# Linear attention: the stage between stick-breaking and the chunk solver is dissolved

## The reference

```python
# stick-breaking group: 8 heads of 64
o = stick_breaking_attention(q, k, v)
o = o * rsqrt(mean(o * o, axis=-1) + RMS_EPS) * sb_out_g           # head norm
# linear group (RWKV-7): 8 heads of 64, token-shifted inputs
r, k, v, xw, xa, xg = split(um)
decay = exp(-exp(-softplus(-(w0 + tanh(xw) @ w2)) - 0.5))
a = sigmoid(a0 + xa @ a2);  g = sigmoid(xg) @ g2                   # g: gates
kk = unit(k * k_k);  k = k * (1 + (a - 1) * k_a)
out = rwkv7_scan(r, decay, k, v, kk, a)    # S = S diag(w) - (S kk)(kk a)^T + v k^T ; o = S r
out = groupnorm(out) * ln_w + ln_b
bonus = sum(r * k * r_k, axis=-1) * v
out = (out + bonus) * g
h = h + concat([o_sb, out]) @ w_out
```

## Time and profile before

| | us |
|---|---|
| runs | 1440.41, 1447.54, 2522.86 (median 1447.54) |
| profiled execution | 1440.73 |
| its span, first to last instruction | 1439.0 |
| TensorE busy | 1280.1 (89%) |
| VectorE busy | 568.4 (40%) |
| ScalarE busy | 479.1 (33%) |
| GpSimd busy | 139.4 (10%) |

### The profile page before, as it was taken

One profiled execution on the slowest core, in us unless ns is written; L12 is line 12 of the kernel. 1 busy time (PEld: TensorE's weight loads), 2 busy tenths in 40 slices (PEclk: granted clock), 3 DMA queues, 4 the chain that ended last, 5 costly groups with the idle time before them and its releaser, 6 DMA issues. The chain is left out here.

```text
span 1439.0 us, 24362 instructions
## 1 busy us (share of the span) xinstructions
PE 1280.1 (89%) x10299; PEld 992.4 (69%) x10299; DVE 568.4 (40%) x1026; ACT 479.1 (33%) x808; POOL 139.4 (10%) x202
## 2 busy tenths in 40 slices
PE   5999979799969589987881999999989979899988
PEld 5886845599848455544441998888867868666668
DVE  3335422655462323321225323444448754522232
ACT  4333366602243301110114234555545534111130
POOL 4000023000000022322210001222100000000000
PEclk9999999999979789998895999999999989999999
DMA  4422000000148579999975545223161035113021
GB/s 147 124 88 88 1 1 0 9 4 4 61 139 320 193 254 389 386 384 394 404 296 185 139 139 103 89 89 91 55 88 59 31 142 184 57 59 117 0 68 50
DMA packets 92488, 195.53 MB, mean 136 GB/s; under 512 B 9510, under 2 KB 73084, under 8 KB 79452
## 3 DMA queue, kind: packets, MB, share of 16 engines
q1 hardware_dynamic: 86604, 183.48, 37.4%
q0 software_dynamic: 5200, 8.40, 1.8%
q10 hardware_dynamic: 576, 2.10, 0.4%
HBM read 184.74 MB, written 16.81 MB: 140 GB/s over the span
## 5 line engine op out<-in xcount | busy, mean ns | idle before, releaser
L1784 PE MATMUL hidden_ps<-w_gate,gathered_t 128*64 128x256 f32 x432 | 116.3, 430 | 24.4 <-DMA w_up<-exp_w_up_dram 24.4
L1784 PE MATMUL hidden_ps<-w_up,gathered_t 128*64 128x256 f32 x432 | 116.3, 430 | 0.0
L1784 PEld LDWEIGHTS hidden_ps<-w_gate,gathered_t 128*64 128x64 f32 x432 | 64.7, 155 | 62.8 <-issue 34.1
L613 DVE TENSOR_TENSOR w_in_low<-w_in_raw,w_in_high 128x2048 fp32r<-128x2048 f32 x20 | 45.8, 2292 | 116.8 <-ACT w_in_high L605 116.8
L565 PE MATMUL proj_ps<-block_in_high,w_in_low 128*128 128x512 f32 x232 | 90.5, 390 | 0.0
L565 PE MATMUL proj_ps<-block_in_low,w_in_high 128*128 128x512 f32 x232 | 90.5, 390 | 0.0
L565 PE MATMUL proj_ps<-block_in_high,w_in_high 128*128 128x512 f32 x232 | 90.4, 390 | 0.0
L1347 PE MATMUL wo_ps<-w_out_high,wo_x_high 128*128 128x256 f32 x256 | 75.2, 294 | 16.6 <-DVE w_out_low L613 16.6
L565 PE MATMUL gate_ps<-block_in_high,gate_w_high 128*128 128x512 f32 x192 | 79.6, 415 | 11.1 <-DVE gate_w_low L613 11.1
L565 PE MATMUL gate_ps<-block_in_low,gate_w_high 128*128 128x512 f32 x192 | 76.6, 399 | 0.0
L565 PE MATMUL gate_ps<-block_in_high,gate_w_low 128*128 128x512 f32 x192 | 76.4, 398 | 0.0
(11 more groups left out here) (457 smaller groups left out, 3102.7 us busy)
## 6 DMA issues: line engine op xcount, KB each, us to landing
w_gate<-exp_w_gate_dram SPq DMA_DIRECT2D x27, 1024.0 KB
w_up<-exp_w_up_dram SPq DMA_DIRECT2D x27, 1024.0 KB
w_down<-exp_w_down_dram SPq DMA_DIRECT2D x27, 1024.0 KB
w_in_raw<-w_in_dram SPq DMA_DIRECT2D x20, 1024.0 KB, 5.6
slot_scratch_and_keys<-w_in_dram SPq DMA_DIRECT2D x14, 1024.0 KB, 5.4
vb<-w_in_dram SPq DMA_DIRECT2D x6, 1024.0 KB, 5.6
gate_w_raw_odd<-w_in_dram SPq DMA_DIRECT2D x6, 1024.0 KB, 5.8
slot_scratch_and_keys<-exp_w_gate_dram SPq DMA_DIRECT2D x5, 1024.0 KB
```

Source lines behind the costliest of these rows:

```text
L613: dve.tensor_tensor(self.part[1][n % 2], self.slot(n), self.part[0][n % 2], ALU.subtract).then_inc(self.low, 1)
L1784: x = pe.matmul(g_bank[e % 2][a * CAP:(a + 1) * CAP, 0:DE], xT[e % 2][:, k, :], w[:, k, :], start=(k == 0), stop=(k == KC - 1))
```

## The change

`rwkv_features` is gone as a stage. Its work goes to four places, in the same amounts:

- First projection: `exps` (ScalarE, behind the split of the last weights) and `operands` (VectorE, behind the keys) form `kr`, the bonus products r k r_k (in place of r) and the scaled keys (in place of k). `kr` lies where the raw weights were, and now keeps all keys ahead of all rows.
- Stick-breaking: VectorE scales `bh` first; TensorE sums the bonus between the scores of head 0 and head 1, in the banks of the values; the norms of output tiles 0 and 1 are computed around heads 5 to 7. Outputs go to `mixT` directly.
- Solver: norms of tiles 2 and 3. The solver's scratch is a tile of its own. The gate weights are loaded here.
- Output stage: the gate matmuls stand behind rounds 1 to 4 of the recurrence, their copies on ScalarE.

`HeadNorm` is a new class with one method for each step of a norm.

```diff
             s.sem("early_" + n) for n in ("lora_product", "sigmoids_stored", "kk_log", "kk_rstd", "vector_step"))
+        self.ex = s.sem("early_decay_exps")
...
         self.step(dve, dve.tensor_tensor(rate, kkn, rate, ALU.mult))
+    def exps(self, act, raw_free):
+        H = self.H
+        act.wait_ge(self.dv, FT + 3)
+        act.activation(H["sig"], H["sig"], ACT.Exp, scale=-DECAY).then_inc(self.ex, 1)
+        act.wait_ge(*raw_free)
+        act.activation(H["kr"][:, 1].rearrange("p i t -> p (i t)"), H["cum"].rearrange("p f t -> p (f t)"), ACT.Exp, scale=-DECAY).then_inc(self.ex, 1)
+        act.activation(H["cum"], H["cum"], ACT.Exp, scale=DECAY).then_inc(self.ex, 1)
+        act.activation(H["mid"], H["ends"], ACT.Exp, scale=-0.5 * DECAY).then_inc(self.ex, 1)
+    def operands(self, dve):
+        H, r = self.H, self.um[:, 0:FT, :]
+        c4 = lambda x: x.rearrange("p f (c t) -> p (f c) t", t=P)
+        dve.wait_ge(self.ex, 1)
+        dve.tensor_tensor(H["kr"][:, 0], c4(H["kkn"]), c4(H["sig"]), ALU.mult).then_inc(self.dv, 1)
+        dve.wait_ge(self.ex, 2)
+        self.n += 1
+        self.step(dve, dve.tensor_tensor(H["kr"][:, 1], c4(r), H["kr"][:, 1], ALU.mult))
+        for f in range(FT):
+            dve.scalar_tensor_tensor(out=r[:, f, :], in0=r[:, f, :], scalar=par_col(self.const, PARAM_AT["rw_r_k"] + f),
+                                     in1=self.k[:, f, :], op0=ALU.mult, op1=ALU.mult).then_inc(self.dv, 1)
+        self.n += FT
+        dve.wait_ge(self.dv, self.n)
+        dve.wait_ge(self.ex, 3)
+        dve.tensor_tensor(self.k, self.k, H["cum"], ALU.mult).then_inc(self.dv, 1)
...
                 wts.split_high(act, FU + 1)
+                early.exps(act, (wts.low, FU + 1))
...
                 early.keys(dve)
+                early.operands(dve)
...
-def stick_breaking(nc, const, qk, v, raw):
+def stick_breaking(nc, const, qk, v, raw, um, R, H):
...
         raw_ready = s.sem("stick_out_ready")
+        norm = HeadNorm(s, const, raw, (0, 1))
+        bz, bonus_st, steps = s.sem("bonus_summed"), s.sem("bonus_ready"), s.sem("steps_ready")
+        vT = um[:, 2 * FT:3 * FT, :]
...
                         pe.wait_ge(raw_ready, f - 1)
+                    else:
+                        pe.wait_ge(bonus_st, FT)
+                    if f == FT - 1:
+                        pe.wait_ge(norm.logged, 1)
...
                 scores(0)
+                for f in range(FT):
+                    if f >= 2:
+                        pe.wait_ge(bonus_st, f - 1)
+                    pe.matmul(avt[f % 2][:, :], const["heads"][:, :], R["bonus"][:, f, :], start=True, stop=True).then_inc(bz, 1)
...
                         scores(h + 2)
+                    if h == NH - 2:
+                        pe.wait_ge(raw_ready, 2)
+                        norm.sum(pe, 0, avt[1][:, :])
+                        pe.wait_ge(w_ready, 3 * (NH - 1))
+                        norm.sum(pe, 1, zt[0][:, 0:S])
...
+                dve.tensor_tensor(R["bh"][:, :, :], R["bh"][:, :, :], H["cum"], ALU.mult).then_inc(steps, 1)
+                for f in range(FT):
+                    dve.wait_ge(bz, f + 1)
+                    dve.tensor_tensor(R["bonus"][:, f, :], avt[f % 2][:, :], vT[:, f, :], ALU.mult).then_inc(bonus_st, 1)
+                mid = R["mid"].rearrange("p (f c) -> p f c", c=NC)
+                dve.tensor_tensor(R["step"], mid[:, :, 0:NC - 1], mid[:, :, 1:NC], ALU.mult).then_inc(steps, 1)
...
                         softplus(h + 1)
+                norm.scale(dve, 0)
+                norm.scale(dve, 1)
...
                         act.activation(raw[:, f, :], avt[f % 2][:, :], ACT.Copy).then_inc(raw_ready, 1)
+                        if f == 1:
+                            act.wait_ge(raw_ready, 2)
+                            norm.square(act, 0)
+                            norm.square(act, 1)
+                    if h == NH - 2:
+                        norm.log(act, 0, avt[1][:, :])
+                        norm.log(act, 1, zt[0][:, 0:S])
+                        norm.inverse(act, 0)
+                        norm.inverse(act, 1)
...
-def rwkv_features(nc, A, const, um, R, H, heads):
...
-def rwkv_chunks(nc, const, um, R, scratch):
+class HeadNorm:
+    def __init__(self, s, const, x, tiles):
+        self.const, self.x, self.first = const, x, tiles[0]
+        self.sq, self.rs = s.sb(f"sbn_sq{tiles[0]}", [P, len(tiles), S]), s.sb(f"sbn_rstd{tiles[0]}", [P, len(tiles), S])
+        self.squared, self.summed, self.logged, self.rstd, self.scaled = (
+            s.sem(f"heads{tiles[0]}_{n}") for n in ("squares", "sums", "logs", "rstd", "scaled"))
+    def square(self, act, f):
+        act.activation(self.sq[:, f - self.first, :], self.x[:, f, :], ACT.Square).then_inc(self.squared, 1)
+    def sum(self, pe, f, out):
+        i = f - self.first
+        pe.wait_ge(self.squared, i + 1)
+        pe.matmul(out, self.const["heads"][:, :], self.sq[:, i, :], start=True, stop=True).then_inc(self.summed, 1)
+    def log(self, act, f, sums):
+        i = f - self.first
+        act.wait_ge(self.summed, i + 1)
+        act.activation(self.rs[:, i, :], sums, ACT.Ln, scale=1.0 / HD, bias=self.const["eps"][:, :]).then_inc(self.logged, 1)
+    def inverse(self, act, f):
+        i = f - self.first
+        act.wait_ge(self.logged, i + 1)
+        act.activation(self.rs[:, i, :], self.rs[:, i, :], ACT.Exp, scale=-0.5).then_inc(self.rstd, 1)
+    def scale(self, dve, f):
+        i = f - self.first
+        dve.wait_ge(self.rstd, i + 1)
+        dve.scalar_tensor_tensor(out=self.x[:, f, :], in0=self.x[:, f, :], scalar=par_col(self.const, PARAM_AT["sb_out_g"] + f),
+                                 in1=self.rs[:, i, :], op0=ALU.mult, op1=ALU.mult).then_inc(self.scaled, 1)
+def rwkv_chunks(nc, A, const, um, R, scratch, heads):
...
         q_st, o_st, m_st, n_st = s.sem("q_stored"), s.sem("o_stored"), s.sem("m_stored"), s.sem("n_stored")
+        norm = HeadNorm(s, const, heads, (2, 3))
+        g2_in = s.sem("lora_g_loaded")
...
         with nc.Block() as block:
+            @block.sync
+            def _(sp):
+                sp.dma_start(R["g2"], A["rw_g2"][0]).then_inc(g2_in, 16)
+                sp.wait_ge(g2_in, 16)
...
                                         m = pe.matmul(sc_bank[r][odd][hs, at:at + 2 * CH], src[head(odd), f, p * P + h * CH:p * P + (h + 1) * CH],
-                                                      R["kr"][head(odd), TT * f + p, :, hs], start=True, stop=True)
+                                                      R["kr"][head(odd), :, TT * f + p, hs], start=True, stop=True)
...
                         ps = slice(p * P, (p + 1) * P)
-                        for j, src in enumerate((R["kr"][:, i, 0, :], vT[:, f, ps], R["bh"][:, f, ps], R["kh"][:, f, ps])):
+                        for j, src in enumerate((R["kr"][:, 0, i, :], vT[:, f, ps], R["bh"][:, f, ps], R["kh"][:, f, ps])):
...
                     pe.wait_ge(tok_st, TT * (f + 1))
+                    if f < 2:
+                        pe.wait_ge(norm.logged, f + 1)
...
                 turn_tokens(0)
+                for f in (2, 3):
+                    norm.sum(pe, f, s_bank[f - 2][:, :])
...
+                norm.square(act, 2)
+                norm.square(act, 3)
                 store_tokens(0)
+                for f in (2, 3):
+                    norm.log(act, f, s_bank[f - 2][:, :])
...
                     store_key_values(2 * i + 1)
+                    if i == 0:
+                        norm.inverse(act, 2)
+                        norm.inverse(act, 3)
...
                         dve.tensor_tensor(by_half(R["q"][:, f, :], h), bank[h][:, :].rearrange("p (c k t) -> p c k t", c=TT, k=2)[:, :, 0, :],
-                                          R["kr"][:, TT * f:TT * (f + 1), 1, hs], ALU.add).then_inc(q_st, 1)
+                                          R["kr"][:, 1, TT * f:TT * (f + 1), hs], ALU.add).then_inc(q_st, 1)
...
                         mask_scores(f + 3)
-def rwkv_output(nc, const, R, mixT, next_w):
+                        norm.scale(dve, 2)
+                        norm.scale(dve, 3)
+def rwkv_output(nc, const, um, R, mixT, next_w):
...
         z_bank = m_bank + v_bank
+        g_bank = [s.ps(f"gate_lora_ps{i}") for i in range(2)]
+        gate_ready, gate_st = s.sem("gate_product"), s.sem("gate_stored")
...
                         m.then_inc(step_ready, 1)
+                    if c <= FT:
+                        if c > 2:
+                            pe.wait_ge(gate_st, c - 2)
+                        pe.matmul(g_bank[(c - 1) % 2][:, :], R["g2"][:, (c - 1) * P:c * P], um[:, 3 * FT + 1, :],
+                                  start=True, stop=True).then_inc(gate_ready, 1)
...
                         dve.wait_ge(fin, 3 * i + 2)
+                        dve.wait_ge(gate_st, i + 1)
...
                 act.preload_act_table_set("natural_log_exp_and_others")
+                for f in range(FT):
```

(24 more changed lines are left out.)

78 lines of the change are left out of this document (removed).

## The result

The changed kernel took 1428.21 us in the median of seven runs (1424.92 to 1430.90), the kernel before 1440.41 beside it. The comparison of the two gives a ratio of 0.9894, with a 95% interval of 0.9878 to 0.9910; it leaves out a slow run of 2522.86 us, one of the seven of the kernel before. The two medians alone would give 0.9915, just outside that interval; by either the changed kernel is about 1% faster, clear of noise. The forecast was 1424.7, range 1417 to 1435, no change of over 2%. The profiled execution took 1426.43 us. The head of its profile shows nearly the same work as before (where TensorE had 1280.1 us, in 24362 instructions of all engines), in a span shorter by 14.4 us: span, instructions, and busy time of each engine.

The account below looks back on a forecast made before the run. The dissolved stage had no full engine and stages ran in series, the solver behind it TensorE's; -18.6 - 1.0 + 0.2 + 3.4 = -16.0 us from the profiled 1440.73 gave 1424.7, range 1417 to 1435.

Parts of the forecast that it names:

- The stage goes, -18.6: Dissolved stage before the solver: the solver begins at 252.44 instead of 271.01, saving 18.6 us.
- First projection, 0: First projection: the added ScalarE and VectorE work costs 0, VectorE's 9.6 us covered by the matmuls of v.
- Start of stick-breaking, -1.0: Stick-breaking's start: softplus 0.5 us late, first suffix 1.64 shorter at full clock; net -1.0, bounds -1.6 and +0.6.
- Norms of tiles 0 and 1, 0: Late stick-breaking: these norms fall into idle time of ScalarE and TensorE, cost 0; 0.3 if ScalarE runs over.
- Start of the solver, +0.2: Solver's start: first scores at full clock -1.6, two norm sums +1.8; net +0.2 us, bounds -1.6 and +1.8.
- the rival by which transposes let the clock fall: Solver's start: sums and second scores run at half speed behind transposes, 3.7 us more, 1428.4; chance 0.03.
- the rival that ended slower: Solver: TensorE held at the low clock, slower than before from 16 us of that work on; chance 0.02.
- Gates, +3.4: Output stage: four gate matmuls between recurrence rounds cost +4.4, shorter rounds save 1.0; net +3.4 us, bounds 0 and +6.8.
- The reading by the busy column: Recurrence rounds: TensorE is full there, so the gates would cost 4.4 us whole, 1.0 more than forecast.
- the first rival: Gates at low clock, first suffix and solver's start cold, all at upper bounds: -9.4 us, so 1431; chance 0.15.
- the gates are not hidden: Denies the rival that TensorE catches up on the gates in the output stage's waits: -19.4 us, 1421.3; chance 0.12.
- VectorE was not late: Denies the rival that VectorE ends the first projection late, waiting on exponentials: up to +9.6 us, 1434; chance 0.04.

Follow-up runs that it names:

- own-stage kernel: Changed kernel with the linear group's exponentials and operands in a separate stage behind the first projection; 1444.21 us beside 1443.89 of the kernel before.
- gates left out: Changed kernel without the four gate matmuls and their copies; first round to output matmuls 5.5 us instead of 10.3, span 1426.5.
- filler: Changed kernel with two more 512-column fp32 matmuls behind head 1's scores, result overwritten; span 1429.6 us.
- norms left out: Changed kernel with all of HeadNorm's calls removed; solver's start to the key values 8.9 us against 10.6, last suffix 5.34 us against 3.68.
- filler at the solver's end: Changed kernel with gates behind variance matmuls, last bonus product behind first softplus, one extra matmul behind head 1's scores, two behind the solver; 1422.03 us, ratio 0.9845.
- gates late: Changed kernel with the gate matmuls moved from the recurrence to behind the variance matmuls, their copies moved too; 1420.29 us in a single run.
- last product late: Changed kernel with VectorE's last bonus product and the chunk steps behind the first softplus instead of ahead; 1420.78 us in a single run.
- the changed kernel again: The changed kernel profiled and timed once more, unaltered; 1430.87 us in six runs, 0.9914 of the kernel before.

## Why the prediction was right

**The stage goes, -18.6.** Right. From stick-breaking's last matmul to the solver's first it is 0.95 us, by the sum 0.97 (252.44 - 251.47). The own-stage kernel shows, for the pieces in the first projection, what the number is made of: it is cover, not work removed.

**First projection, 0.** Right. VectorE ended at 181.26 (forecast 181.0), and ScalarE had 1.73 us left. I had called it wrong if stick-breaking started later than 183.3; it started at 183.55 in one execution and at 182.73 in the other of the same kernel, so that bound was narrower than what executions differ by. With the cover taken away, stick-breaking starts 11.5 us later; my bound of 9.6 left out that VectorE must also wait for the first exponential (1.9 us).

**Start of stick-breaking, -1.0.** This is the term that was wrong in the profiled execution, and right in the next. The delay of the softplus was 0.65 us, not 0.5. The clock I took as a function of the idle gap: "5.77 to about 2.0", so it stays. The gap was shorter still, 1.42, and the clock fell in one execution and not in the other. From the first scores to the solver the first took 70.0 us, the second 68.4; the kernel before's 68.4 to its last matmul make 69.4 with the same boundary. So +0.6 in one and -1.0 in the other: my upper bound and my forecast. That the forecast was met in the second is partly luck, as the gap had not settled it. In four other executions (gates left out, filler, norms left out, filler at the solver's end) the clock also fell behind the 0.94 us at the boundary, which none of my bounds had: with the gates left out, where this stage is unaltered, it took 71.7 us, so +2.3.

**Norms of tiles 0 and 1, 0.** Right, and more: they fill a gap behind which the clock fell once, for 1.7 us, in two executions without them.

**Start of the solver, +0.2.** Right: 12.60 us to the levels (266.11 - 253.51), where it was 12.39. The first scores and the transposes behind them ran at full clock, so the rival by which transposes let the clock fall did not come about. The Trainium skill ("TensorE: Matmul & The Clock Gate", Part 4) says that the full clock doesn't come with transposes. This trace disagrees: the two sums behind the transposes took 1.81 us, and the rival had them and the second scores 3.7 us longer. Nor did the solver lose its clock, the rival that ended slower: from its start to the first round it is 116.4 us (369.87 - 253.51), where it was 116.1.

**Gates, +3.4.** The mechanism was right, the size was not: 4.7 in the profiled execution. The rounds and waits behind them, with my +3.4 spread over the rows:

| | forecast | measured |
|---|---|---|
| round 1 | 0.89 | 0.61 |
| gate 1 | 1.7 | 1.65 |
| round 2 | 0.89 | 1.05 |
| gate 2 | 0.91 | 1.59 |
| round 3 | 0.5 | 0.61 |
| gate 3 | 0.91 | 1.05 |
| round 4 | 0.5 | 0.62 |
| gate 4 | 0.91 | 1.05 |
| rounds 5 and 6, and the wait behind | 1.8 | 2.1 |

The clock fell after the first round, at about 371, and not before it, so a second gate fell into the low stretch (0.7). A gate takes 1.05 us from its start to the next round's, not the 0.91 of a stream of its own kind. A round takes 0.61 until the gate starts, not 0.5. These 0.1 us each I had left out; no run shows their cause. The second execution took 10.26 us, with a first gate of 2.01 and a second of 1.20; the three at full clock took 8.73, so +3.1. My 3.4 lies between the two prices, and it had the low stretch in it: with one there it was too low by 1.3.

The Trainium skill ("Perfetto Trace Analysis", Identifying the Most-Contended Engine), with which I had sided, says that matmul busy time is a bad measure of headroom. It says so of how near a kernel is to its peak, not of the price of one more matmul in a chain. The reading by the busy column, 4.4, was the nearer one to 4.7, though not for its reason: the rounds did get shorter.

**The rest.** Up to the output projection the sum comes out, with start and clock put right: -18.6 - 1.0 + 0.2 + 4.7 = -14.7, and the second execution of the changed kernel has 399.4 - 414.2 + 0.3 (its earlier start) = -14.5. Behind it I had called the prediction wrong if stages changed their length by over 3 us. They do, by 3.4 us here and from execution to execution, so by my own sign this part was wrong. From the output projection's first copy to the second block's first projection it is 378.3 us in the kernel before, 374.9 and 379.7 in two executions of the changed kernel, and 376.6 to 380.2 in the others, over code and data that are the same. Why this stretch varies stays open; no run here was made for it.

The first profiled execution adds up so: to -16.0 come 0.5 (a later start of stick-breaking), 1.6 (the clock at the first suffix) and 1.3 (gates), less 1.8 behind the output projection, where nothing was changed: -14.4. Without those 1.8 the forecast would have been 3.4 off and not 1.6; that is luck. The forecast of 1424.7 lay 3.5 us under the median of the runs, and the first rival's 1431 only 2.8 over it. The time alone can't tell the two; the traces can, against that rival: the solver started at full clock, and two of the four gates ran at it. The other rivals fall as well: the gates are not hidden, and VectorE was not late.

## What to carry to other kernels

A stage with no full engine is worth dissolving for the length it has on the clock of the whole, 18.6 us here, but only if each piece lands under work that doesn't wait for it: price the pieces by what is idle there, as the own-stage run shows that 9.6 us of them, uncovered, delay the next stage by 11.5. A matmul put between the rounds of this recurrence is paid in full, 0.9 us each at full clock; the same four behind it, ahead of their first reader, cost 0.3 together. Before calling 1 or 2 us an effect, profile the same kernel twice.

## What the hardware showed that I had not expected

Over these lengths, TensorE's clock did not follow from the idle gap in front. Nine profiled executions of the changed kernel and its variants start stick-breaking behind a gap of 0.94 us; in four of them the clock went to 0.50 some 2 to 3 us later, with TensorE busy since. Five of the nine have the 1.42 us gap before the first suffix; in three the clock fell behind it, among them one of two executions of the same instructions. A gap of 2.25 us was harmless in the kernel before and cost 1.7 us with the norms left out. Behind the 2.46 us in front of the recurrence the clock was at 0.50 for a part of the rounds in seven executions, the kernel before included, and at 1.00 throughout in three.

Where a filler closed the gap before the first suffix, that suffix ran at 1.00 in each of the three kernels that had one. Without a filler it did so in three of seven (gates late, last product late, the changed kernel again), so three out of three is a hint and not a proof. Behind the next gap, 0.91 or 0.92 us, the clock still fell in one of the three. What decides between the two levels behind such short gaps stays open here.
